# Where the rests of the normalised tokens begin in a partition: 64 bytes further

## The reference

```python
for l in range(DEPTH):
    h = h + 0.5 * _swiglu(_rmsnorm(h, ffn1_norm[l]), ffn1_w1[l], ffn1_w3[l], ffn1_w2[l])
    u = _rmsnorm(h, mix_norm[l])
    z = u @ w_in[l]                      # q, k, v of three branches, forget logits, gates
    ...
    m = (gates[:, :, 0] * (o_a @ proj_a[l]) + gates[:, :, 1] * (o_b @ proj_b[l])
         + gates[:, :, 2] * (o_c @ proj_c[l]))
    h = h + m @ w_out[l]
    h = h + 0.5 * _swiglu(_rmsnorm(h, ffn2_norm[l]), ffn2_w1[l], ffn2_w3[l], ffn2_w2[l])
return _rmsnorm(h, final_norm)
```

## The kernel before

| array | start before | by 128 | start after | by 128 |
|---|---|---|---|---|
| h | 1152 | 0 | 1152 | 0 |
| u_hi | 17536 | 0 | 17536 | 0 |
| u_lo | 33920 | 0 | 33984 | 64 |
| w_raw | 50304 | 0 | 50432 | 0 |
| v_area | 68736 | 0 | 68864 | 0 |
| scratch | 81024 | 0 | 81152 | 0 |
| area | 97408 | 0 | 97536 | 0 |
| w_hi | 196160 | 64 | 196288 | 64 |
| w_lo | 211520 | 64 | 211648 | 64 |
| cst | 227456 | 0 | 227584 | 0 |

## Time and profile before

### The profile page before, as it was taken

The page is one execution under the profiler, slowest core; times in us unless marked ns, Lnnn a source line. Parts: engine busy times, 40 slices in busy tenths (PEclk is TensorE's granted clock), DMA queues, the critical chain, the costliest instruction groups (busy, mean ns, idle before and its releaser), DMA issues.

```text
span 2415.4 us, 48244 instructions
## 1 busy us (share of the span) xinstructions
PE 2400.3 (99%) x15594; PEld 2200.2 (91%) x15594; DVE 2116.3 (88%) x3964; ACT 1498.9 (62%) x2948; POOL 3.2 (0%) x10
## 2 busy tenths in 40 slices
PE   9999999999999999999999999999999999999999
PEld 8999888999889889998889998888888998899988
DVE  8999878999898779998699997789998986899986
ACT  6666358888755456664466663578886554566644
POOL 0000000000000000000000000000000000000000
PEclk9999999999999999999999999999999999999999
DMA  4333332212232323333333323322212333233332
GB/s 162 110 106 105 114 102 65 77 56 78 62 114 92 102 88 107 108 112 114 109 95 107 104 96 106 113 71 62 73 60 71 105 113 97 88 105 107 118 109 84
DMA packets 64675, 233.46 MB, mean 97 GB/s; under 512 B 7168, under 2 KB 7552, under 8 KB 64512
## 3 DMA queue, kind: packets, MB, share of 16 engines
q1 hardware_dynamic: 64368, 231.32, 29.5%
q10 hardware_dynamic: 144, 0.11, 0.0%
HBM read 229.30 MB, written 2.10 MB: 96 GB/s over the span
## 4 chain that ended last, share of the span: by engine, by line
PE 82%; DVE 11%; issue 4%; ACT 2%; DVEq 1%; DMA 0%; ACTq 0%; SPq 0%
PE ps L753 23%; PE ps L754 23%; PE ps L755 23%; DVE w_lo L2084 3%; PE ps L1004 3%; PE ps L1073 2%; PE ps L1055 2%; PE ps L1057 2%; PE ps L1056 2%; PE ps L1027 2%; DVE area L2084 1%; ACT w_hi L1337 1%; DVE w_raw L2207 1%; DVE scratch_whole L2220 1%; DVE w_raw L2215 1%
## 5 line engine op out<-in xcount | busy, mean ns | idle before, releaser
L1337 ACT ACTIVATE w_hi<-w_raw 128x512 fp32r<-128x512 f32 (+2 forms) x888 | 624.0, 714 | 485.6 <-PE ps L755 194.9
L2084 DVE TENSOR_TENSOR w_lo<-w_raw,w_hi 128x512 fp32r<-128x512 f32 (+2 forms) x888 | 699.8, 796 | 90.5 <-ACT w_hi L1337 74.3
L753 PE MATMUL ps<-u_hi,w_hi 128*128 128x256 f32 (+1 forms) x2240 | 704.6, 315 | 0.0
L755 PE MATMUL ps<-u_hi,w_lo 128*128 128x256 f32 (+1 forms) x2240 | 702.0, 313 | 0.0
L754 PE MATMUL ps<-u_lo,w_hi 128*128 128x256 f32 (+1 forms) x2240 | 701.9, 313 | 0.0
L754 PE MATMUL ps<-area,w_hi 128*128 128x256 f32 (+1 forms) x1778 | 581.3, 327 | 0.0
L753 PE MATMUL ps<-area,w_hi 128*128 128x512 f32 (+1 forms) x1414 | 483.4, 342 | 5.8 <-ACT scratch_whole L1443 4.4
L755 PE MATMUL ps<-area,w_lo 128*128 128x512 f32 (+1 forms) x1414 | 479.1, 339 | 0.0
L753 PEld LDWEIGHTS ps<-u_hi,w_hi 128*128 128x128 f32 x2240 | 420.7, 188 | 28.6 <-DVE w_lo L2084 1.0
L755 PEld LDWEIGHTS ps<-u_hi,w_lo 128*128 128x128 f32 x2240 | 420.8, 188 | 28.4
L754 PEld LDWEIGHTS ps<-u_lo,w_hi 128*128 128x128 f32 x2240 | 420.7, 188 | 27.7
(11 more groups left out here) (208 smaller groups left out, 3155.0 us busy)
## 6 DMA issues: line engine op xcount, KB each, us to landing
w_raw<-weights SPq DMA_DIRECT2D x432, 512.0 KB, 3.7
h<-x SPq DMA_DIRECT2D x4, 512.0 KB, 6.6
out<-scratch_whole SPq DMA_DIRECT2D x8, 256.0 KB, 2.0
scratch_whole<-const_b SPq DMA_DIRECT2D x1, 256.0 KB, 9.0
scratch_whole<-const_r SPq DMA_DIRECT2D x1, 192.0 KB, 8.4
cst<-const SPq DMA_DIRECT2D x1, 143.0 KB, 8.4
par<-params ACTq DMA_DIRECT2D x1, 105.0 KB, 4.4
```

Of the source, the lines that this page charges most:

```text
L753: pe.matmul(dst, hi, x_hi, start=start, stop=False, **kw)
L755: return pe.matmul(dst, lo, x_hi, start=False, stop=stop, **kw)
L1337: return act.activation(dst, src, ACT.Copy)
L2084: return dve.tensor_tensor(dst, src, hi_part.bitcast(F32), ALU.subtract)
```

## The change

Two arrays of 16 float32 columns (64 bytes of each partition), which nothing reads or writes, are put ahead of `u_lo` and behind it. `u_lo` so begins 64 bytes further, and all arrays behind it 128 bytes further. No instruction is added, removed or moved on any engine; only addresses change.

```diff
         h = sb("h", ND * SEQ)
         u_hi = sb("u_hi", ND * SEQ, F32R)
+        sb("gap2", 16)
         u_lo_whole, u_lo = sb_two("u_lo", ND * SEQ)
+        sb("gap3", 16)
         w_raw = sb("w_raw", RAWS * UNIT * P)
         rstd = sb("rstd", SEQ)
```

## The result

| | before | changed |
|---|---|---|
| median of 7 runs, us | 2413.98 (2412.53 to 2416.31) | 2422.27 (2422.03 to 2423.52) |
| the profiled execution, us | 2417.53 | 2422.73 |
| its span, us | 2415.4 | 2420.6 |

The ratio is 1.0033, 95% interval 1.0024 to 1.0043: 8.3 us, outside the range of the prediction. In a later sitting the two stood at 2421.92 and 2414.73, ratio 1.0030 (1.0018 to 1.0042). The changed kernel's runs lie closer together (1.5 us) than before's (3.8 us).

The account below looks back on a forecast made before the run. The prediction took the number of matmuls times their pace as the bound (TensorE busy 2400.3 of 2415.4 us), with small stops where VectorE is late. All terms were 0, so the median stays at 2413.2 us; range 2407 to 2421.

Parts of the forecast that it names:

- TensorE streaming from `u_lo`: Matmuls streaming `u_lo` while weights at remainder 64 load: 0 forecast, bounded by 4.4 ns either way for each.
- the 384-column pair: Score matmuls (338 ns) and L1056 (337 ns), whose stream and load remainders are 0/0 and 64/0; source of the forecast 0.
- 4.4 ns either way, since one pace step is the smallest and only step seen: Bound for each matmul that touches `u_lo`, from the difference between two paces seen at 256 and 512 columns.
- All other arrays: moved by 128 bytes ... I take 0: Arrays behind `u_lo` keep their remainder by 128; their distance to `h` and `u_hi` grows by 128: 0 forecast.
- the instant at which a wait ends: Claimed to choose which of two paces a TensorE stretch takes and keeps until its next stop; 4.4 ns per matmul apart.
- +-1.3 us: Estimated spread if half of some 100 stretches outside the loops chose their pace anew at random.
- The loop: Loop of hidden pairs: VectorE sets the 19.87 us turn, the slow pace leaves about 0.08 us of room; turn unchanged.
- The sign that the prediction gave for a changed turn: If the loop's turn left 19.87 us, VectorE's operations would have changed length, which was put at nothing.
- faster rival: Unlike remainders let token matmuls outside the loops take the fast pace; loops give nothing: 10 us less, 2403, chance 0.09.
- VectorE's writes, loads from `u_lo` and transfers at 0: VectorE writes to `u_lo`, L1056 loading it as weights (at most 1.1 us either way), and transfers: each taken as 0.
- slower rival: Stream and load on the same 64-byte half cost each matmul streaming `u_lo` 4.4 ns: 7 us, 2420, chance 0.17.
- its sign in the profile: Unequal starts in a `u_lo` product, longer after L754, L754's mean up 3 ns or more, L753's on `area` unchanged.

Follow-up runs that it names:

- all_at_distance_64: Before with the gap ahead of `w_hi` at 56 columns for 24, so both weight arrays lie 64 bytes past tokens and `area` modulo 256: 2420.28 us, ratio 1.0015.
- rest_at_0: Before with one 32-column gap behind `u_lo`: `u_lo` stays at remainder 0, all later arrays move by 128 bytes: 2417.81 us against 2416.88, ratio 1.0007.
- both_at_64: Before with 16-column gaps ahead of `u_hi` and behind `u_lo`: both token arrays at remainder 64, later arrays 128 bytes further: 2419.97 us, ratio 1.0013.
- rest_at_192: Before with gaps of 48, 16, 16 columns: modulo 256, `u_lo` 192 past `u_hi`, weights 0, `area` 64: 2412.83 us against 2414.73, ratio 0.9995.

## Why the prediction was wrong

**The step that failed** is "TensorE streaming from `u_lo`", and in it the value: "I take 0, the value of the 384-column pair". What it measured in the trace: with 512 columns a matmul of a token product takes 2.3 ns more on average, 1989 x 2.3 = 4.6 us; with 256 outside the loop 1.8 ns, 1054 x 1.8 = 1.9 us; in the loop 36 turns x 0.02 us = 0.7 us. That is 7.2 us where the prediction has 0. It is a sum over the two profiled executions, whose spans differ by 5.2 us: 1.7 us more come from the narrow matmuls on `area` (see "Still open"), together 8.9 of the 9.6 us by which TensorE is busier, and 4.4 us of waiting fall away. That it equals the smaller of the two differences of medians, 7.2 and 8.3 us, is chance. The 384-column pair was the wrong neighbour: it is a third width, and the two widths that matter here answer the same distance with opposite signs (at distance 0, 226.7 ns is the best of 512 columns and 120.0 among the worst of 256). And L1004 was the same relation for `u_lo` alone: its stream and load are at distance 0 modulo 256, and so are the new `u_lo` and the weights. But `u_hi`, which streams in two of the three matmuls, went from distance 192 to 64 with the weights' 128 bytes, and such a mixed triple stood in none of the rows at 256 or 512 columns.

**The bound in that step**, "4.4 ns either way, since one pace step is the smallest and only step seen", was too small and wrong in kind. For each matmul that streams `u_lo` it was 3 x 2.3 = 7 ns with 512 columns and 3 x 1.8 = 5 ns with 256 outside the loop, since its neighbours pay too. And two paces are not all that there are: the bare matmuls show 226.7, 228.9, 232.5, 233.3 and 234.4 ns. Unequal steps by themselves were no sign, as before's fast pace has them too. That 256 columns of `u_hi` also went up (279 to 282 ns) was outside the thought: I priced the matmuls that touch `u_lo`, but the three matmuls of a triple set the pace together.

**"All other arrays: moved by 128 bytes ... I take 0"** was right in the sum and wrong in the reason. 128 bytes take the tokens' distance to the weights from 192 to 64: with the rest kept at 0, that is 231.0 to 233.0 ns at 512 columns and 116.9 to 116.2 at 256, which nearly cancel (ratio 1.0007). The 392-column weights on which I leaned move up to 2.5 ns between groups and versions (177.1 to 179.6) and decide nothing. So the two terms put at 0 one by one were not independent: with the weights kept `u_lo`'s place costs 2.5 us, with `u_lo` kept the weights' place 0.9 us (not to be told from 0), and both together more than either.

**The choice of pace by "the instant at which a wait ends"** holds only inside one set of starts. The starts first fix which paces exist, one (226.7 and 120.0 at distance 0) or two (113.3 and 117.8 at 64, with 256 columns). Rows 4 and 5 were also not quite the same operands: rows 4 end on `v_area`, rows 5 stay on `area`, both at distance 192. The "+-1.3 us" of chance had the right size: the standard deviation of before's runs within a sitting is 1.1 to 1.4 us. That it comes from the choice of pace is not shown. Before scatters by 3.8 to 5.3 us between its fastest and slowest run and every other version, with fewer runs, by 0.5 to 2.3, among them all_at_distance_64 (2.0) and rest_at_0 (1.4), which have two paces as well. Before's medians in four sittings, 2413.98, 2416.88, 2416.46 and 2414.73, differ by sitting and partly by chip, so only ratios within a sitting count.

**The loop** before was read rightly: VectorE sets its turn, and a slower pace first eats the room of 0.08 us. In the changed kernel the pace eats more than the room, and 96 x 118.7 + 72 x 117.9 ns = 19.88 us, against 19.89 measured. The sign that the prediction gave for a changed turn, that VectorE's operations had changed length, was wrong: they kept it, and TensorE became the one that sets the turn. The same sum gives 96 x 120.1 + 72 x 118.0 = 20.03 us for both_at_64, as measured, and the fast pace of all_at_distance_64 gains nothing there, as the faster rival's text said of the loops.

**VectorE's writes, loads from `u_lo` and transfers at 0**: nothing in the trace after contradicts it (751 ns, 338 ns, DMA 0% of the chain).

**The slower rival**, at 0.17 and 2420 us, had the size and the sign, and its sign in the profile came: unequal steps, the longest behind the matmul on `u_lo` (236.0 ns), its mean up by 3 ns with 512 columns (2 with 256) and `area`'s not. That was luck, for its rule was wrong all the same, and so were its terms: 2 us in the loops and 4.8 outside, where 0.7 and 6.5 were measured. One half for everything is the fastest place at 512 columns, and moving only the weights (all_at_distance_64) costs 4.2 ns on `area` at 512 columns without any pair in one half that was not before. Its price of 4.4 ns for L754 alone was in truth 7 ns, spread over the triple: mostly 708 or 698 ns for 700 or 687. The Trainium skill's sentence that separate ports keep loads and streams apart (TensorE: Matmul & The Clock Gate, Step-by-step: what each phase is for) was a reason to rate it low; whatever the ports do, the weights' start changes the pace of the stream here. The gap of columns / 2.4 + 2.5 ns, the other thing that the prediction took from that page of the Trainium skill (section Back-to-back issue gap), stands there for an isolated matmul and not for a row of loads and matmuls. That the rows lie above it was no argument for this rival.

**The faster rival** asked whether leaving the common remainder frees the fast pace; it is the other way round: no place with the rest off hi's has 113.3 ns, and of those twelve only (128, 128) and (192, 0) keep 228.9.

**Still open.** The narrow matmuls on `area` outside the loop went from 116.4 to 117.3 ns (1878 x 0.9 = 1.7 us) although their distances are kept. The changed kernel's second trace, on another chip, has 117.2, and the three other versions on the first chip that keep these distances have 117.3 to 117.5; rest_at_192 has 116.4. So it repeats, and chance alone is an unlikely cause. A part of it stands in the second projections beside triples that mix arrays: `v_area` with `u_lo` went from 115.6 to 118.5 ns, and the triples on `area` alone from 115.9 to 117.1. Whether the pace of a stretch follows from what stands ahead of it was not tested. How much distances matter at 384 columns was not measured with bare matmuls; in the kernels the groups of that width lie between 172.6 and 177.7 ns. Nor do the runs show what in the memory or in TensorE makes the 256-byte period.

## What to carry to other kernels

When TensorE is busy nearly all the time (99% here) with matmuls that each load their weights, the starts of the stream and of the loaded block modulo 256 bytes are a tuning parameter of up to 3% at 512 columns and 6% at 256 (226.7 against 234.4 ns, 113.3 against 120.7), and the best value differs by width. Measure it with a small program of bare matmuls at the real addresses, in triples as the kernel issues them: it gave the kernels' paces within 2 ns. Give the hi part and the rest of one operand the same place modulo 256 bytes, unless such a program shows another to be as good, and choose the distance to the weights by the width that has the most matmuls outside stops. Count each width, and take off what a loop bound by another engine hides. The gain can be small: no version here was clearly faster than before, whose distance of 192 is second best at 512 columns.

## What the runs showed of the hardware that was not expected

- The distance from start to start of back-to-back fp32r matmuls with a load each, at the full granted clock: 226.7, 228.9, or 230 to 234.4 ns with 512 columns and 113.3, or 117 to 120.7 with 256, when only the starts of the operands differ, on zeros; the kernels' means on real data follow within 2 ns.
- The dependence on the weights' start has a period of 256 bytes (moved by 0 to 480 bytes). Distance 0 is the best at 512 columns (226.7) and among the worst at 256 (120.0).
- A stretch can have more than one stable pace at the same starts (113.3 and 117.8) and keeps the one it fell into.
- Three matmuls in a row set their pace together: with the rest and the weights 64 past hi 234.4 ns, where the sum of the single distances would be 231.2.
